# Forming C times the S5 coefficients in the GLA layer, and one memory tile of the S5 layer at the GLA layer's end

## The chip, the cores and the metric

The kernel runs on one core of a Trainium2 chip. The metric is the device time of one execution in microseconds (us); lower is better. The core has five engines with queues of their own: TensorE (PE, with its weight loads shown as PEld), VectorE (DVE), ScalarE (ACT), GpSimd (POOL) and SyncE (SP), which issues most DMAs. PE writes to PSUM (8 banks of 512 f32 columns on 128 partitions), the others work between PSUM and SBUF. They wait for each other through semaphores that are written out by hand in the kernel.

## What is computed

A batch of 256 tokens of width 1024 goes through a first block (attention, mLSTM, a mixture of 32 experts) and then through a second block of two layers, GLA (gated linear attention) and S5 (a diagonal state-space model), each with attention over 256 memory tokens beside it. The change touches the second block. Its reference, cut:

```python
mem_n = rms_norm_2(mem, mem_norm_w)
for i in range(2):                                   # 0: GLA, 1: S5
    h = rms_norm_2(x, norm_w[i])
    seq_out, z, xq = gla_branch(h, ...) if i == 0 else s5_branch(h, ...)
    xa = memory_attention(xq, mem_n, xa_w_kv[i])     # k, v = split(mem_n @ w_kv)
    y = concatenate([seq_out, xa], axis=-1) * silu(z)
    x = x + y @ w_out[i]
...
# s5_branch: u, z, xq = split(h @ w_in)
dt = exp(log_step); mag = exp(lam_re * dt)
ab = mag * (cos(lam_im * dt), sin(lam_im * dt))      # 128 groups x 64 states
coef = (ab - 1) / lam                                # complex
bb = coef * B                                        # B: 64 x 16 per group
x_t = ab * x_{t-1} + bb * u_t
y_t = Re(C x_t) + d * u_t                            # C: 16 x 64 per group
y = gelu(y); y = y * sigmoid(y @ w_glu + b_glu)
```

## The kernel before

The weights of the dense products come in tiles of 2 MB ([128, 4096] f32), numbered in order of use and streamed by SP through a ring of three slots (`RING`); tile n may be loaded once `tile_done` says that tile n - 3 has been used. The ranges of the numbers are `T_GLA` (14 tiles), `T_GLA_OUT` (6), `T_S5` (16), `T_GLU` (8), `T_S5_OUT` (6). Each stage is a `Block` with one hand-written program for each engine; at its end all engines meet at a barrier.

**GLA layer (`stage_gla_layer`).** Most of its input projection and all of the output projections are made as Strassen products: a tile is 7 products of 4 matmuls, and an engine forms sums of quarters of the weight tile first (`sum_weights`, four 128x1024 operations; POOL does so for the input tiles, DVE for the output tiles) and sums of the rows (`dve_rows`, four 128x512 operations). A matmul instruction of the program shows as two in the profile. Behind the input tiles come halves of tiles by plain products (`half`, lines L1846), each 16 matmul instructions into one PSUM bank (6 or 7), taken out by ACT. DVE normalises and gates the attention output (`normalise`, L2126; the gating, L2143), PE turns it (L188), DVE copies it out (L2149). Then the memory attention: scores (L1949), maxima and exponentials, scaling of p by DVE (L2162), turning of p (L1957), its product with `vm` (L1964), multiplication into `zT` (L2169). Between these PE runs the six tiles of the output projection (`out.pe_tile`, L1686). Tiles 2 and 3 need the row sums of the third k block, which DVE can form only after the memory attention. DVE forms the weight sums of tiles 2 to 5 in this stretch, and between those of tiles 3 and 4 it computes the S5 coefficients (`a["decay"]`, `a["turns"]`, `a["coef"]`, lines L2175 to L2215, 64 columns each) with Exp and Sin from ACT (L2033 to L2037). PE turns `ab` behind tile 4 (L1974), ACT stores it to DRAM (`s5_ab_rows`), and the stage ends with the norm for the next layer: squares on ACT (`act_squares`, L1724), roots on POOL (`pool_rstd`), scaling on DVE (L2222), 16 transposes on PE (L1980), and DVE's multiplication into `hT` (L2227).

**S5 scan (`stage_s5_scan`).** 16 steps q; each handles 8 groups of 16 channels, two time steps folded into one. Beside them PE makes the layer's input projection: 32 halves (16 tiles, of which 4 are keys and values of the memory), two a step, one in steps 14 and 15 (`halves_of`). On PE a step is: `half`, `bu(q + 1)` (input times B, L2354), `skip_product(q)` (L2364), second `half`, `y(q)` (states times C, L2373 and L2377). `y(q)` waits for DVE's rotation (`rotated`) and its masked skip matrix (`skip_ready`, L2501). DVE: rotation of bu by the tables (L2474 to L2477), the next step's `step_in` (L2452 to L2455) and `fraction` (L2442), 8 scans (L2487, L2488), `take_y(q - 1)` (L2461), rotation back (L2492 to L2499), skip mask. ACT makes the tables of sine and cosine and takes out the halves. POOL forms `cb`, C times the coefficients, from raw C: four 128x256 operations and one of 128x512 (L2315 to L2320), double buffered, so that group q waits for `y(q - 2)`. SP loads B (with the broadcast `s5_ab_rows`), C (128 KB) and B by state two steps ahead, in that order, and then the ring's next tile.

## Time and profile before

| | us |
|---|---|
| median of 3 runs | 1561.13 (1558.21 to 1562.0) |
| the profiled execution | 1563.43, span 1561.7 |
| mean granted TensorE clock | 0.991 |
| GLA layer | 760 to 1080 |
| S5 scan | 1080.58 to 1363.20 |
| S5 output stage | 1363.20 to the end |

Busy shares of the span: PE 97%, PEld 63%, DVE 44%, ACT 19%, POOL 11%. The first block takes the first 760 us. Read a row of the timeline as: start from the span's start, length of the merged group, engine, line, operation, output and inputs, shapes, count, and in brackets the engine's idle time ahead of it with what ended it. Ends of matmuls are modelled, so a start is surer than an end. PE's granted clock is 1.00 (2.4 GHz) nearly everywhere; 0.50 is 1.2 GHz.

### The profile page before, as it was taken

To read this page: it belongs to the slowest core of one execution; us is meant where nothing else is said; L and a number is where in the kernel's file an instruction comes from. 1 tells how busy PE (TensorE), PEld (TensorE's weight loads), DVE (VectorE), ACT (ScalarE), POOL (GpSimd) and SP (SyncE) were. 2 spreads that over 40 slices of the span, in tenths; PEclk is the share of its full clock that TensorE was granted. 3 is DMA by queue.
4 is the path that set the end of the run, shared out by engine and by line. 5 is a ranking of instruction groups with operands and counts; after the bars stand their busy time and mean duration, and the time that the engine had idled before them with its cause. 6 is when DMAs were issued, how large, how long until landed. Compare 5 with 4: busy or idle time off the path is not lost. (4 is left out here: it accounts for less than half of the span.)

```text
span 1561.7 us, 22744 instructions
## 1 busy us (share of the span) xinstructions
PE 1508.0 (97%) x9125; PEld 989.6 (63%) x9125; DVE 692.0 (44%) x1313; ACT 289.7 (19%) x556; POOL 169.3 (11%) x161
## 2 busy tenths in 40 slices
PE   6999999999999999999999999998999999899998
PEld 2475655344444434433478688887888887488887
DVE  2544324111111111111633333473788888895663
ACT  2222202111111211111120030101223232230000
POOL 0000000000000000000636420002121122000000
PEclk9999999999999999999999999999999999999999
DMA  9544639899999999999333244244454344233441
GB/s 399 213 162 162 254 126 418 337 421 422 422 422 422 422 422 422 422 422 423 118 126 144 108 162 161 109 149 151 142 185 148 136 173 162 111 123 134 164 167 48
DMA packets 53890, 376.05 MB, mean 241 GB/s; under 512 B 7216, under 2 KB 18224, under 8 KB 19264
## 3 DMA queue, kind: packets, MB, share of 16 engines
q1 hardware_dynamic: 53536, 374.02, 60.3%
q8 instruction: 46, 0.75, 0.2%
q10 hardware_dynamic: 288, 1.11, 0.2%
q14 instruction: 20, 0.16, 0.0%
HBM read 373.99 MB, written 1.11 MB: 240 GB/s over the span
## 5 line engine op out<-in xcount | busy, mean ns | idle before, releaser
L1246 PE MATMUL ps<-ring,x_gathered 128*64 128x512 f32 x1024 | 227.9, 597 | 1.0 <-DVE x_gathered L1311 0.9
L1320 DVE TENSOR_TENSOR act_slots<-gate,ps 64x512 f32<-64x512 f32 x32 | 22.1, 690 | 381.3 <-ACT gate L1284 381.3
L2340 PE MATMUL ps<-hT,ring 128*128 128x256 f32 x768 | 172.4, 383 | 2.4 <-PEq L115 2.4
L1246 PEld LDWEIGHTS ps<-ring,x_gathered 128*64 128x64 f32 x1024 | 73.9, 138 | 148.9 <-issue 147.1
L2340 PEld LDWEIGHTS ps<-hT,ring 128*128 128x128 f32 x768 | 145.3, 192 | 23.8 <-issue 4.6
L1269 PE MATMUL ps<-ring,act_turned 128*64 128x512 f32 x512 | 116.9, 598 | 0.0
L1269 PEld LDWEIGHTS ps<-ring,act_turned 128*64 128x64 f32 x512 | 33.9, 136 | 79.1 <-issue 54.8
L1224 PE MATMUL ps<-y,selT 64*128 64x512 f32 x264 | 75.0, 634 | 0.7 <-ACT y L1290 0.7
L261 PE MATMUL ps<-ring,hT 128*128 128x512 f32 x160 | 69.8, 593 | 0.0
L1686 PE MATMUL ps<-ring,zT 128*128 128x256 f32 x288 | 67.4, 380 | 1.9 <-DVE glu_by_token L1548 1.3
L1213 PEld LDWEIGHTS ps<-sel,h 128*128 128x128 bf16 x1584 | 48.4, 98 | 29.1 <-issue 26.0
L1686 PEld LDWEIGHTS ps<-ring,zT 128*128 128x128 f32 x288 | 54.2, 190 | 10.3 <-DVE glu_by_token L1548 1.7
L1379 POOL TENSOR_SCALAR end_stat<-end_ss 128x1 f32<-128x1 f32 x2 | 0.9, 469 | 516.8 <-ACT ring L1369 516.8
L1846 PE MATMUL ps<-hT,ring 128*128 128x256 f32 x256 | 55.7, 379 | 0.0
L1213 PE MATMUL ps<-sel,h 128*128 128x64 bf16 x1584 | 52.3, 194 | 2.4 <-DVE sel_weighted L1301 2.4
L1284 ACT ACTIVATE gate<-ps 64x512 f32<-64x512 f32 x32 | 18.9, 591 | 187.6 <-PE ps L1246 187.6
L2442 DVE SCALAR_TENSOR_TENSOR s_sin<-const,s_turns,s_sin 128x128 f32<-128x128 f32 x64 | 42.8, 727 | 23.1 <-ACT s_sin L2405 23.1
L261 PEld LDWEIGHTS ps<-ring,hT 128*128 128x128 f32 x160 | 29.9, 190 | 35.8 <-issue 35.8
L1846 PEld LDWEIGHTS ps<-hT,ring 128*128 128x128 f32 x256 | 48.5, 190 | 6.5
L1290 ACT COPY y<-ps 128x512 f32<-128x512 f32 x32 | 18.7, 586 | 132.4 <-PE ps L1269 132.4
L280 PE MATMUL ps<-ring,crep 128*32 128x512 f32 x192 | 26.5, 675 | 11.4 <-DMA ring<-in_weights 11.4
L1591 PE MATMUL ps<-ring,hT 128*128 128x256 f32 x144 | 34.6, 383 | 1.4 <-DVE o_sq L1622 1.4
(637 smaller groups left out, 2383.8 us busy)
## 6 DMA issues: line engine op xcount, KB each, us to landing
ring<-in_experts SPq DMA_DIRECT2D x192, 1024.0 KB, 17.1
ring<-in_weights SPq DMA_DIRECT2D x75, 2048.0 KB, 7.7
b_raw<-in_s_b SPq DMA_DIRECT2D x16, 128.0 KB, 7.2
s_a_rows<-s_ab_rows SPq DMA_DIRECT2D x64, 32.0 KB, 6.6
c_raw<-in_s_c SPq DMA_DIRECT2D x16, 128.0 KB, 6.2
b_by_state<-in_s_b_by_state SPq DMA_DIRECT2D x16, 128.0 KB, 2.0
x<-in_x ACTq DMA_DIRECT2D x1, 1024.0 KB, 5.0
mix_room<-in_mem SPq DMA_DIRECT2D x1, 1024.0 KB, 13.9
```

Source lines behind the costliest of these rows:

```text
L261: last = pe.matmul(bank, src[:, kk, h * P:(h + 1) * P], w[:, kk, :], start=(kk == 0), stop=(kk == KD - 1))
L280: last = pe.matmul(bank[32 * j:32 * j + 32, :], crep[:, 2 * j + i, :], w[:, 2 * j + i, :], start=(i == 0), stop=(i == 1), skip_group_check ...
L1213: last = pe.matmul(xg_ps[:, f, :], a["h2"][:, t, part, f * P:(f + 1) * P], sel[:, t, :], start=(t == 0 and part == 0), stop=(t == TT - 1 a ...
L1224: last = pe.matmul(acc[:, t, n, :], selT[rows, b, t * P:(t + 1) * P], y[rows, :], start=False, stop=stop, skip_group_check=True)
L1246: last = pe.matmul(h_ps[rows, :], xg[:, f, :], w[:, kk, m, :], start=(f == 0), stop=(f == KD - 1))
L1269: last = pe.matmul(y_ps[rows, :], act_t[:, f, :], w[:, kk, n * 512:(n + 1) * 512], start=(f == 0), stop=(f == 3))
L1320: dve.tensor_tensor(act_s[:], gate[:], h_ps[upper, :], ALU.mult).then_inc(act_ready, 1)
L1591: last = pe.matmul(self.ps(bank, h), rows[:, kk, :], w[:, kk, :], start=(start and h == 0 and kk == 0), stop=(kk == 3), skip_group_check=True)
L1686: last = pe.matmul(self.sum_of(n, p), rows[:, kk, :], w[:, kk, :], start=(first and kk == 0 and self.PLACE[p][1] == 0), stop=(self.ends(i) ...
L1846: last = pe.matmul(bank[:, f, :], w[:, kk, (2 * h + f) * P:(2 * h + f + 1) * P], k.hT[:, kk, :], start=(kk == 0), stop=(kk == KD - 1))
L2340: last = pe.matmul(out[:, f, :], w[:, kk, (2 * h + f) * P:(2 * h + f + 1) * P], rhs[:, kk, :], start=(kk == 0), stop=(kk == KD - 1))
L2442: last = dve.scalar_tensor_tensor(out=sin[b][:, j, :], in0=even, scalar=a["turns"][:, 4 * q + j:4 * q + j + 1], in1=sin[b][:, j, :], op0=A ...
```

## The change

1. The S5 coefficients are computed earlier in the GLA layer: ACT's part before it takes out the plain halves, DVE's around the gating.
2. POOL's work on C moves from the scan into the GLA layer, behind its weight sums. Raw C is loaded in three DMAs: 1 MB into `hT` when the last input tile is done, and two of 512 KB into parts of `gla_v` after the memory attention. POOL writes to four buffers, and ACT stores each group (256 KB) to DRAM (`s5_c_bar`). In the scan SP loads the finished groups into three buffers.
3. The tile order changes: the first key tile of the S5 layer becomes tile `T_S5`, and its two halves run at the GLA layer's end (`keys_half`), one ahead of the transposes, one behind. ACT takes them out.
4. The scan has 30 halves: two a step, one in steps 3, 7, 11 and 15. `y(q - 1)` stands behind the first half of step q; the rotated states are double buffered, and DVE's `take_y` stands behind the wait for the skip product.

```diff
-T_GLU = T_S5 + 16
+T_S5_SCAN = T_S5 + 1
+T_GLU = T_S5_SCAN + 15
...
             def _(sp):
-                stream(k, sp, T_END_FIRST, T_S5)
+                stream(k, sp, T_END_FIRST, T_GLA_OUT)
+                for h, q in ((0, 0), (1, 8), (2, 12)):
+                    n = 8 if h == 0 else 4
+                    if h == 1:
+                        load(T_GLA_OUT + RING)
+                        sp.wait_ge(xa_out, 1)
+                    sp.dma_start(c_raw[h], k.dram["s5_c"][q:q + n].rearrange("q p j c g -> p q j c g")).then_inc(c_in[h], 16)
+                for n in range(T_GLA_OUT + RING + 1, T_S5_SCAN + RING):
+                    load(n)
                 sp.wait_ge(ab_out, 16)
+                for b in range(4):
+                    sp.wait_ge(c_out[b], 16 * 4)
...
             def _(pe):
+                def keys_half(i, bank):
+                    out, w = k.ps[:, bank, :].rearrange("p (f t) -> p f t", f=2), k.slot(T_S5)
+                    for f in range(2):
+                        for kk in range(KD):
+                            last = pe.matmul(out[:, f, :], w[:, kk, (2 * i + f) * P:(2 * i + f + 1) * P], k.memT[:, kk, :],
+                                             start=(kk == 0), stop=(kk == KD - 1))
+                    return last
...
                 out.pe_tile(pe, 5)
+                k.wait_tile(pe, T_S5)
+                keys_half(0, 1).then_inc(keys_done, 1)
                 pe.wait_ge(ab_copied, 1)
                 for j, t in enumerate((1, 0)):
                     pe.wait_ge(s5_scaled, j + 1)
+                    if t == 0:
+                        pe.wait_ge(keys_out, 1)
...
+                pe.wait_ge(out.added, 4)
+                keys_half(1, 4).then_inc(k.tile_done, 1)
...
             def _(act):
-                out.act_squares(act, 0)
+                for q in range(16):
+                    if q == 10:
+                        out.act_squares(act, 0)
+                    act.wait_ge(c_ready, q + 1)
+                    act.dma_start(k.dram["s5_c_bar"][q], c_bar[:, q % 4].rearrange("p c e j g -> p (c e j g)")).then_inc(c_out[q % 4], 16)
                 act.wait_ge(ab_turned, 1)
...
                 out.act_squares(act, 1)
+                for i, (bank, sem, value) in enumerate(((1, keys_done, 1), (4, k.tile_done, T_S5 + 1))):
+                    act.wait_ge(sem, value)
+                    act.activation(kmT[:, 2 * i:2 * i + 2, :], k.ps[:, bank, :].rearrange("p (f t) -> p f t", f=2),
+                                   ACT.Copy).then_inc(keys_out, 1)
...
             def _(pool):
+                pool.wait_ge(coef_ready, 1)
+                for q in range(16):
+                    pool.wait_ge(c_in[0 if q < 8 else q // 4 - 1], 16)
+                    b = q % 4
+                    if q >= 4:
+                        pool.wait_ge(c_out[b], 16 * (q // 4))
...
+                    pool.tensor_tensor(c_bar[:, b, 0], c_re, cr, ALU.mult)
+                    pool.tensor_tensor(c_bar[:, b, 1], c_re, neg_ci, ALU.mult)
+                    pool.tensor_tensor(c_tmp[:, 0], c_im, neg_ci, ALU.mult)
+                    pool.tensor_tensor(c_tmp[:, 1], c_im, neg_cr, ALU.mult)
+                    pool.drain()
+                    pool.tensor_tensor(c_bar[:, b], c_bar[:, b], c_tmp[:], ALU.add).then_inc(c_ready, 1)
+                    pool.drain()
                 out.pool_rstd(pool)
...
 def stage_s5_scan(k, a):
-        halves_of = [[2 * q + 2, 2 * q + 3] for q in range(14)] + [[30], [31]]
+        starts = [2 + 7 * (q // 4) + 2 * (q % 4) for q in range(17)]
+        halves_of = [list(range(starts[q], starts[q + 1])) for q in range(16)]
...
-                        sp.wait_ge(cb_ready, q + 1)
+                        if q:
+                            sp.wait_ge(y_done, q)
                         load_c(q + 2)
...
                     half(now[0])
+                    if q:
+                        y(q - 1)
                     if q < N - 1:
                         bu(q + 1)
                     skip_product(q)
                     for i in now[1:]:
                         half(i)
-                    y(q)
+                y(N - 1)
...
                     dve.drain()
-                    if q:
-                        take_y(q - 1)
                     dve.tensor_tensor(e_re, z_re[:], cos[b][:], ALU.mult)
...
                     dve.wait_ge(skip_done, q + 1)
+                    if q:
+                        take_y(q - 1)
                     dve.tensor_tensor(skip[:], k.ps[:, 4 + b, 2 * S:3 * S], own[:], ALU.mult).then_inc(skip_ready, 1)
```

The instructions as they stand in a row on the engines, at three places. PE at the GLA layer's end, before: the last products, the 16 transposes of the normalised rows (`gla_v`), and the scan's first two halves.

```order
L1686 MATMUL ps<-exp_k,zT 128x256 x4
L1686 MATMUL ps<-ring,rows_gla_bias 128x256 x4
L1686 MATMUL ps<-ring,zT 128x256 x4
L1980 MATMUL ps<-const,gla_v 128x128 x16
L1817 UNCONDITIONAL_BRANCH
L2323 UNCONDITIONAL_BRANCH
L2340 MATMUL ps<-hT,ring 128x256 x32
```

And with the change (`memT` are the memory tokens):

```order
L1687 MATMUL ps<-exp_k,zT 128x256 x4
L1687 MATMUL ps<-ring,rows_gla_bias 128x256 x4
L1687 MATMUL ps<-ring,zT 128x256 x4
L1898 MATMUL ps<-memT,ring 128x256 x16
L2015 MATMUL ps<-const,gla_v 128x128 x16
L1898 MATMUL ps<-memT,ring 128x256 x16
L1825 UNCONDITIONAL_BRANCH
```

A half of the key tile stands on each side of the transposes. PE in the scan's last two steps, before: half 30, bu(15), skip(14), y(14), half 31, skip(15), y(15).

```order
L2334 MATMUL ps<-ring,memT 128x512 x8
L2354 MATMUL ps<-uT,ab_bar 128x128 x4
L2354 MATMUL ps<-uT,b_raw 128x128 x4
...
L2364 MATMUL ps<-c_bar,b_by_state 128x128 x2
L2373 MATMUL ps<-uT,skip 128x128
L2377 MATMUL ps<-s_x_re,c_bar 32x128 x8
L2377 MATMUL ps<-s_x_im,c_bar 32x128 x8
L2334 MATMUL ps<-ring,memT 128x512 x8
L2364 MATMUL ps<-c_bar,b_by_state 128x128 x2
```

With the change, from y(13) on:

```order
L2419 MATMUL ps<-uT,skip 128x128
L2423 MATMUL ps<-s_x_re,c_bar 32x128 x8
L2423 MATMUL ps<-s_x_im,c_bar 32x128 x8
L2400 MATMUL ps<-uT,ab_bar 128x128 x4
L2400 MATMUL ps<-uT,b_raw 128x128 x4
...
L2410 MATMUL ps<-c_bar,b_by_state 128x128 x2
L2380 MATMUL ps<-ring,memT 128x512 x16
L2419 MATMUL ps<-uT,skip 128x128
```

Two halves now stand between bu(15) and y(14). POOL in the GLA layer, with the change: the last weight sums, the roots, and the first of 16 groups; before, the roots of the next norm (`pool_rstd`) followed at once.

```order
L1468 TENSOR_TENSOR ring<-ring 128x4x256
L1470 TENSOR_TENSOR zT<-ring,zT 128x1024
L179 TENSOR_SCALAR o_rstd<-o_ss 128x8
L182 TENSOR_TENSOR o_rstd<-o_rstd,const 128x8
L2104 TENSOR_TENSOR c_bar_out<-hT,s_coef 128x256
L2105 TENSOR_TENSOR c_bar_out<-hT,s_coef 128x256
L2106 TENSOR_TENSOR c_tmp<-hT,s_coef 128x256
L2107 TENSOR_TENSOR c_tmp<-hT,s_coef 128x256
L2109 TENSOR_TENSOR c_bar_out<-c_bar_out,c_tmp 128x512
```

The 80 operations stand between the attention's roots and the roots of `pool_rstd`, on which the transposes wait.

## Rows read from the trace of the kernel before

**Rows 1.** PE timeline, GLA end: start, us, engine, line, operation, [idle before <-releaser].

```profile
1075.01 1.07 PE L1980 MATMUL ps<-const,gla_v 128*128 128x128 f32 x8 [1.60 <-DVE gla_v L2222]
...
1080.58 0.67 PE L2340 MATMUL ps<-hT,ring 128*128 128x256 f32 x2 [2.37 <-PEq L115]
```

**Rows 2.** PE timeline in one scan step: y, half tile, next half tile.

```profile
1113.05 0.39 PE L2373 MATMUL ps<-uT,skip 128*128 128x128 f32 x2
...
1114.38 7.17 PE L2340 MATMUL ps<-hT,ring 128*128 128x256 f32 x32
...
1123.16 7.07 PE L2340 MATMUL ps<-hT,ring 128*128 128x256 f32 x32
```

**Rows 3.** PE timeline at the scan's end and the next stage's start.

```profile
1348.51 0.79 PE L2373 MATMUL ps<-uT,skip 128*128 128x128 f32 x2 [4.14 <-DVE skip L2501]
...
1351.10 8.90 PE L2334 MATMUL ps<-ring,memT 128*128 128x512 f32 x16
...
1360.83 0.49 PE L2373 MATMUL ps<-uT,skip 128*128 128x128 f32 x2 [0.39 <-DVE skip L2501]
...
1363.20 7.14 PE L2548 MATMUL ps<-kmT,s_xqT 128*128 128x256 f32 x32 [0.87 <-PEq L2266]
```

**Rows 4.** DVE timeline: starts of steps 0 and 1, last rotation of step 15.

```profile
1097.61 0.69 DVE L2474 TENSOR_TENSOR s_z_re<-ps,s_cos 128x512 f32<-128x512 f32 x1 [10.18 <-PE ps L2354]
...
1110.83 0.69 DVE L2474 TENSOR_TENSOR s_z_re<-ps,s_cos 128x512 f32<-128x512 f32 x1 [0.17 <-issue]
...
1358.88 0.68 DVE L2499 TENSOR_TENSOR s_x_im<-s_x_im,s_t_im 128x512 f32<-128x512 f32 x1
```

**Rows 5.** Windows view, scan start: busy us by engine, PEclk, DMA share, GB/s.

```profile
1082.00:1084.00 2.00, 2.00 (x7) 1.55 (x6) 1.14 (x4) 0.79 (x2) 0.00 (x0) 0.50 0.30 70
```

**Rows 6.** PE timeline: three idle times and the matmuls behind them.

```profile
225.61 1.75 PE L990 MATMUL ps<-memT,ring 128*128 128x256 f32 x7 [1.80 <-PEq L366]
...
760.83 8.77 PE L1841 MATMUL ps<-ring,hT 128*128 128x512 f32 x16 [2.12 <-PEq L115]
...
793.88 2.83 PE L1591 MATMUL ps<-zT,hT 128*128 128x256 f32 x8 [2.92 <-DVE gla_qk L1629]
```

**Rows 7.** Timeline: DVE and POOL operations that overlap, GLA layer and scan.

```profile
769.20 2.83 DVE L1488 TENSOR_TENSOR gla_xqT<-hT 128x512 f32<-128x512 f32 x1
...
816.74 2.35 POOL L1464 TENSOR_TENSOR zT<-ring 128x1024 f32<-128x1024 f32 x1 [7.66 <-PE ps L1591]
...
819.23 3.15 POOL L1466 TENSOR_TENSOR zT<-ring,zT 128x1024 f32<-128x1024 f32 x1
...
820.24 3.22 DVE L2084 TENSOR_TENSOR gla_qk<-gla_qk,gate_state 128x1024 f32<-128x1024 f32 x1
...
1336.89 2.90 DVE L2442 SCALAR_TENSOR_TENSOR s_sin<-const,s_turns,s_sin 128x128 f32<-128x128 f32 x4 [1.49 <-ACT s_sin L2405]
```

**Rows 8.** POOL timeline: first and last operation of one group of c_bar.

```profile
1090.05 0.61 POOL L2315 TENSOR_TENSOR c_bar<-c_raw,s_coef 128x256 f32<-128x256 f32 x1 [0.16 <-issue]
...
1092.53 1.26 POOL L2320 TENSOR_TENSOR c_bar<-c_bar,c_tmp 128x512 f32<-128x512 f32 x1
```

**Rows 9.** Timeline at the GLA output projection, ACT, DVE and PE.

```profile
983.26 0.60 ACT L1988 ACTIVATE gla_xqT<-ps 128x512 f32<-128x512 f32 x1 [6.31 <-PE ps L1846]
...
997.76 2.19 DVE L2162 TENSOR_SCALAR gla_v<-gla_v,xa_rs 128x256 f32<-128x256 f32 x8
...
1003.01 1.91 PE L1957 MATMUL ps<-const,gla_v 128*128 128x128 f32 x16
...
1023.29 0.68 DVE L1488 TENSOR_TENSOR zT<-zT 128x512 f32<-128x512 f32 x1
...
1024.05 1.59 PEld L1686 LDWEIGHTS ps<-ring,zT 128*128 128x128 f32 x8 [0.54 <-issue]
...
1048.89 1.97 PE L1686 MATMUL ps<-ring,zT 128*128 128x256 f32 x8 [0.40 <-DVE exp_q L1469]
```

**Rows 10.** The page's DMA issues: KB each, median us to landing.

```profile
ring<-in_weights SPq DMA_DIRECT2D x75, 2048.0 KB, 7.7
```

## What the change should do to the time

> **What bounds the kernel now.** Read first which engine never rests: in the table of the profile it is TensorE (PE), busy 97% of the span, and what it waits for is what can be won. So the second view is PE's idle time in the GLA layer's end and the S5 scan, the two places that the diff touches. There are two large holes. The first lies between the GLA layer's last product and the scan's first matmul: PE stops at 1073.4 (1075.01 less its 1.60 of idle), turns the normalised rows in two short bursts, and starts the scan at 1080.58 [rows 1]: 7.2 us with little work in them. The second is at the scan's end, where y(14) waits 4.14 us for DVE's `skip` [rows 3]. Inside the scan PE does not wait: y takes 1.33 us (1113.05 to 1114.38), and the half tile behind it, with bu and the skip product, 8.78 (to 1123.16) [rows 2]; half a tile is 6.9 to 7.1 us, so bu and the skip product are 1.7. A step with two halves is then some 17.0 us.
>
> The third view is the granted clock. After the first hole it reads 0.50, the 1.2 GHz level, at 1082 to 1084 [rows 5]. After the second, half(31) takes 8.90 us [rows 3] against 7.07 [rows 2], and y(14) takes 2.59 (1348.51 to 1351.10) against 1.33.
>
> **The GLA layer's front (coefficients moved up).** DVE's block of 64-column operations and ACT's Exp and Sin move from the output projection to the gating. PE there runs half tiles of 6.9 us each and asks for the gated rows later than DVE gives them, so I cost the move at nothing; if that cover failed it would cost at most the 4 us of DVE work put ahead of the gating. ACT's takes of the halves come 2 us late at worst, under the same half tiles.
>
> **One tile leaves the scan.** Two halves, 2 x 6.9 = 13.8 us, go. The sum over the scan stage has one more part, the tail. Before, it lost 4.1 (idle) + 1.3 (y at half clock) + 1.8 (half(31), 8.90 less 7.07) + 0.4 (1360.83) = 7.6 us [rows 3]. After, two halves and y(14) stand between bu(15) and y(15): 0.5 + 2 x 6.9 + 1.3 + 0.5 = 16.1 us, while DVE's last step takes 11.1 (from 1348.5, when it had released PE, to 1359.56) [rows 3, 4]. So DVE's rotation is in time, and only take_y(14) and the skip product's mask, which now stand behind the skip product, are waited for: some 0.9 us, an estimate. Gain of the tail 6.7. Scan stage: 13.8 + 6.7 = **20.5 us less**.
>
> The short steps (3, 7, 11) take PE 17.0 - 6.9 = 10.1 us while a DVE step takes 13.2 (1097.61 to 1110.83) [rows 4]. I still cost them at nothing: y is now behind the next step's first half, so DVE has a full step and a half (25 us after bu) and two steps, one long and one short, give 27 us for 26.4 of DVE. SP's loads: b is issued at the end of a step and used 12 us later, C (now 256 KB) a step and a half ahead.
>
> **The tile's two halves in the GLA layer's end.** From the last product to the scan's first matmul there will be 2 x 6.9 for the halves, 2 x 0.9 for the turns, and then the stage boundary behind a PE and ACT finish, which at the layer's start shows 2.12 us of idle [rows 6], with 0.2 for hand-overs: 17.9 against 7.2, so **10.7 us more**. The clock fall at the scan's start stays: after the 2.12 us at 760.83 the 16 matmuls took 8.77 us, where such a half takes 7.1.
>
> **C times the coefficients on POOL.** One group took 1090.05 to 1093.79, with the drain 3.9 us [rows 8]; 16 groups are 62 us. They can't begin before the raw C has landed in `hT`, which is free at 983.3 (the last take) [rows 9]; a 2 MB tile is ahead of it, at 7.7 us [rows 10], and 1 MB more lets me set 994 (bounds 991 and 1002). So POOL works from 994 into the 1070s, beside DVE's weight and row sums.
>
> That isn't free. DVE's operation on two SBUF tensors at 769.20 took 2.83 us [rows 7], the same 512 columns 0.68 at 1023.29 [rows 9]; at 820.24 one of 1024 columns took 3.22, while POOL's at 819.23 was stretched from the 2.35 of the one at 816.74 to 3.15 [rows 7]. Start and end times show turns: DVE waits until POOL's operation has ended, then POOL waits for DVE. Against short c_bar operations four small DVE operations took 2.90 us, 0.73 each [rows 7]. The Trainium skill (SBUF — State Buffer, Who interferes with whom) has the rule behind it: the port pair of VectorE and GpSimd is an exclusive lock, held for the whole instruction, when the DVE operation has two SBUF inputs or runs in a 2-port mode. By its "whole instruction" POOL would lose every such DVE operation in full; the row at 819.23 shows 0.8 us lost for one of 1.2. By the rule the sixteen weight-sum operations would move POOL's end, below, from 1074 to about 1079, still inside its cover; the sum goes by the row.
>
> On PE's path this has three prices. (a) The eight scalings of p: 8 x 0.73 = 5.8 from 997.76 is 1003.6, PE wants them at 1003.01 [rows 9]: **0.6** (bounds 0 and 2.5). (b) The four row sums before tile 2: PE already waits for their end (1023.29 + 0.68, PE at 1024.05 with 0.54 of idle) [rows 9], so all of it lands. Each waits for one POOL operation, a fifth of 3.75 us, less what overlaps: 4 x 0.6 = **2.4** (bounds 0, and 4 x 2.15 = 8.6 by the row at 769.20; POOL's operations are a quarter as long here, so I stay near the low end). (c) PE is then idle 2.9 us. Idle of 1.80 us left the clock alone, 2.12 and 2.92 were followed by a fall [rows 6], and a fall cost 1.7 to 1.8: **1.8** (bounds 0 and 3.1, the two losses behind the second hole). The weight sums: 4 x (1.1 + 0.75) = 7.4 us against 4.9; DVE no longer does the 10 us of coefficients between them, PE's tiles are 12 us apart, and even 9 us would hide. The 0.4 us that tile 4 waited for DVE [rows 9] goes. Together 0.6 + 2.4 + 1.8 - 0.4 = **4.4 us more**.
>
> POOL's end: 994 + 62 + 16 weight-sum operations x 0.8 to 1.0 + some 3 for the rest, about 1074. ACT's queue holds the copy of `ab` and the last squares behind the sixteenth store, and POOL's own roots come behind its last group; PE needs these at about 1085 (1073.4 + 4.4 + 6.9), and they take some 4 us, an estimate. So the last group may end at 1081: 7 us of cover.
>
> **Sum.** -20.5 + 10.7 + 4.4 = -5.4 us. The profiled execution took 1563.43 us for a span of 1561.7, 2.3 above the median of 1561.13; the change should take it to 1558.0 and the median to **1555.7 us**.
>
> **Rivals.**
> *The port costs PE nothing* (C lands late, or the turns fall well): the 2.4, 0.6 and 1.8 are gone, 10.2 less in all: 1550.9. Against it: the row sums have no cover at all. A half-way case, the port without the clock fall, is 1553.9.
> *POOL is late, slower than before.* If the last group ends after 1081, each us delays ACT's copy, the squares and the roots, and with them the turns and the scan. It decides from 1081 and eats the whole gain at 1086 to 1087, that is at 5.8 us a group from 994, where I expect 5.0; at 1092 the kernel takes 1566.7. For it: 3.9 us is the time with DVE quiet, and each store must have left before a buffer is used again. Against it: 7 us of cover.
> *Short steps wait for DVE.* If ACT's tables (which wait for PE's half) hold DVE up in the short steps, PE stands still 2 to 4 us at up to four places: the tail's gain of 6.7 is given back and 2 more: 1564.
> *The change doesn't do what it says*: PE's hole is filled, but the scan isn't shorter, since DVE bounds it. Against it: a DVE step of 13.2 us stands against a mean of 15.3 for PE (three long steps, one short). It is counted in the case before.
>
> **Chances.** Forecast with its half-way case 0.60; port free 0.17; POOL late 0.13; short steps 0.10. A measurement tells about 0.3% (4.7 us) from no change. The forecast lies just beyond that: of its 0.60 some 0.38 is faster by more, 0.22 within. With the port-free case faster is 0.55. Of the two slow cases, 0.23, a mild half (0.11) stays within; so same 0.33, slower 0.12. The range takes in the port-free case with 1.4 us beyond it and the milder part of the slow ones: 1549.5 to 1561.5.
>
> **What would show it.** Tile 2 of the output projection starts some 3 us later, with 2.5 to 3.5 us of PE idle before it and a clock of 0.50 behind. DVE's 128x512 row sums there take 1.2 to 1.4 us each, its 1024-column sums 1.8. POOL's last group ends between 1070 and 1080. From the last product to the scan's first matmul 18 us; the scan stage 262 us instead of 282.6 (1080.58 to 1363.20 [rows 1, 3]), with no PE wait but 1 us before y(15). I am wrong if PE waits for `ab_copied` or the scaled rows by several us, if PE waits in steps 3 to 12, or if DVE's row sums keep their 0.68 us.

## The result and the profile after

The changed kernel takes 1546.12 us (median of 4 runs, 1544.83 to 1548.01), beside 1559.67 for the kernel before in the same comparison: a ratio of 0.9907, 95% interval 0.9894 to 0.9919, so 14.5 us faster by the ratio. A second measurement of the same pair (after_again, below) gave 0.9899, 0.9882 to 0.9916. The forecast was 5.4 us, and 1555.7 us with a range from 1549.5: the sign was right, the size was not.

The two profiled executions differ by more than the medians, by 18.0 us of span (1561.7 and 1543.7). So the first step is to cut the span where both kernels do the same. Three points serve: the first matmul of the GLA layer's memory scores, the scan's first matmul, the first matmul of the S5 output stage.

| us | before | after | difference | forecast |
|---|---|---|---|---|
| start to the scores | 983.91 | 980.41 | -3.50 | 0 |
| scores to the scan's first matmul | 96.67 | 107.33 | +10.66 | +15.1 |
| scan | 282.62 | 257.48 | -25.14 | -20.5 |
| output stage to the end | 198.50 | 198.48 | -0.02 | 0 |

The first line is not the change's. 3.3 us of it are there at the first large product, 36 us into the program, where no line differs. PE timeline of the first 40 us, before:

```profile
33.84 5.23 PE L411 MATMUL ps<-hT,w_gate 128*4 128x256 f32 x32 [1.60 <-DVE hT L699]
39.00 20.87 PE L261 MATMUL ps<-ring,hT 128*128 128x512 f32 x48
```

and after:

```profile
32.13 3.62 PE L412 MATMUL ps<-hT,w_gate 128*4 128x256 f32 x32 [1.60 <-DVE hT L700]
35.69 20.87 PE L262 MATMUL ps<-ring,hT 128*128 128x512 f32 x48
```

The same 32 matmuls took 5.23 and 3.62 us: in one execution the clock was still at its lower level. The 980 us ahead of the scores varied by 8.7 us in the twelve executions below (975.21 to 983.91). The S5 coefficients, moved up in the GLA layer, cost PE nothing, as forecast: from the layer's first product to the scores it is 223.08 us before (760.83 to 983.91) and 223.11 after (757.30 to 980.41). The change's own share of the profiled pair is 10.66 - 25.14 - 0.02 = -14.5 us, and this is what the rest explains. Lines of the changed kernel are numbered 1 to 48 higher.

**The GLA layer's end** (PE timeline), against [rows 1]: the key tile's halves stand on both sides of the transposes.

```profile
1070.04 7.07 PE L1898 MATMUL ps<-memT,ring 128*128 128x256 f32 x32
1076.95 2.01 PE L2015 MATMUL ps<-const,gla_v 128*128 128x128 f32 x16
1078.79 7.07 PE L1898 MATMUL ps<-memT,ring 128*128 128x256 f32 x32
1087.74 14.05 PE L2386 MATMUL ps<-hT,ring 128*128 128x256 f32 x64 [1.88 <-PEq L116]
```

From the end of the last product to the scan's first matmul it is 1087.74 - 1070.2 = 17.5 us. Behind the 1.88 us of idle the clock did not fall: 64 matmuls took 14.05 us. The windows view (length, busy us and count by engine, PEclk, DMA share, GB/s) of the stretch that answers to [rows 5] reads 1.00:

```profile
1088.00:1090.00 2.00, 2.00 (x11) 1.74 (x11) 0.23 (x1) 1.66 (x5) 0.00 (x0) 1.00 0.89 369
```

**The port**, against [rows 9]. DVE timeline: scalings of p, then the four row sums before tile 2.

```profile
994.26 5.07 DVE L2264 TENSOR_SCALAR gla_v<-gla_v,xa_rs 128x256 f32<-128x256 f32 x8
...
1017.65 0.69 DVE L1484 TENSOR_TENSOR gla_xqT<-zT 128x512 f32<-128x512 f32 x1
1018.41 0.95 DVE L1486 TENSOR_TENSOR gla_xqT<-gla_xqT,zT 128x512 f32<-128x512 f32 x1
1019.44 0.95 DVE L1488 TENSOR_TENSOR gla_xqT<-zT,gla_xqT 128x512 f32<-128x512 f32 x1
1020.31 1.10 DVE L1489 TENSOR_TENSOR zT<-zT 128x512 f32<-128x512 f32 x1
```

PE's turning of p began at 999.50, right behind its matmuls. What is left of the port on PE's path is one wait, ahead of tile 2 (PE timeline, before):

```profile
1024.08 1.97 PE L1686 MATMUL ps<-ring,zT 128*128 128x256 f32 x8 [0.16 <-issue]
```

and after:

```profile
1021.51 1.97 PE L1687 MATMUL ps<-ring,zT 128*128 128x256 f32 x8 [1.10 <-issue]
```

**POOL's end** (POOL timeline: last operation of the last group, last root):

```profile
1069.62 1.27 POOL L2109 TENSOR_TENSOR c_bar_out<-c_bar_out,c_tmp 128x512 f32<-128x512 f32 x1
...
1075.00 0.55 POOL L182 TENSOR_TENSOR gla_out_rstd<-gla_out_rstd,const 128x1 f32<-128x1 f32 x1
```

The second half of the rows was scaled at 1076.33 (DVE, 1075.58 and 0.75 us); PE wanted it at 1077.9, in the middle of the transposes.

**The scan.** PE timeline of one long step, against [rows 2]:

```profile
1111.62 13.98 PE L2386 MATMUL ps<-hT,ring 128*128 128x256 f32 x64
1125.43 0.39 PE L2419 MATMUL ps<-uT,skip 128*128 128x128 f32 x2
...
1126.77 0.51 PE L2400 MATMUL ps<-uT,ab_bar 32*128 32x128 f32 x8
...
1128.44 13.98 PE L2386 MATMUL ps<-hT,ring 128*128 128x256 f32 x64
```

The step is 1128.44 - 1111.62 = 16.82 us, where it was 1131.40 - 1114.38 = 17.02. A short step is 9.9 us. PE does not wait in any of them; it waits once, before y(15), where [rows 3] had 4.14 us before y(14):

```profile
1342.85 0.49 PE L2419 MATMUL ps<-uT,skip 128*128 128x128 f32 x2 [0.77 <-DVE skip L2549]
```

### The profile page after: what moved, and what is told of

Its sections match the earlier page's. It is cut to its first block and busy times, and to the rows that moved or that the text cites. A ratio compares the mean times of both kernels' runs of the same rounds, so it can differ in the third digit from the quotient of the medians.

```text
span 1543.7 us, 22762 instructions
## 1 busy us (share of the span) xinstructions
PE 1496.5 (97%) x9125; PEld 987.0 (64%) x9125; DVE 680.3 (44%) x1313; ACT 293.9 (19%) x559; POOL 184.2 (12%) x161
## 3 DMA queue, kind: packets, MB, share of 16 engines
q10 hardware_dynamic: 2592, 5.31, 0.9%
HBM read 378.19 MB, written 5.31 MB: 248 GB/s over the span
## 5 line engine op out<-in xcount | busy, mean ns | idle before, releaser
L2386 PE MATMUL ps<-hT,ring 128*128 128x256 f32 x768 | 168.3, 379 | 1.9 <-PEq L116 1.9
L1868 PE MATMUL ps<-hT,ring 128*128 128x256 f32 x256 | 55.7, 379 | 0.0
```

What stands on the lines that cost most here:

```text
L1868: last = pe.matmul(bank[:, f, :], w[:, kk, (2 * h + f) * P:(2 * h + f + 1) * P], k.hT[:, kk, :], start=(kk == 0), stop=(kk == KD - 1))
L2386: last = pe.matmul(out[:, f, :], w[:, kk, (2 * h + f) * P:(2 * h + f + 1) * P], rhs[:, kk, :], start=(kk == 0), stop=(kk == KD - 1))
```

## Experiments

First theory, from these rows: 14.5 = 5.4 forecast + 9.1, and the 9.1 are 4.1 of the port's price that PE never paid, 1.7 of a clock fall at the scan's start that did not come, 2.9 in the scan, where 14 steps of before lost 0.2 us each, and 0.3 at the GLA end. The rival for each: that the term was small by luck of one execution, or that something else gave the time.

Whole times are too coarse for this: the part before the scores varies. So each experiment is judged by its stages in the trace. They repeat well, as the two executions of the changed kernel show (after_again is the same kernel once more). Each is a difference of three start times of PE's timeline and the span, in us. The last two columns are of whole executions; before was measured anew beside each group of kernels.

| kernel | scores at | scores to scan | scan | output stage | median | ratio to before, interval |
|---|---|---|---|---|---|---|
| before | 983.91 | 96.67 | 282.62 | 198.50 | 1559.67 to 1561.93 | 1 |
| after | 980.41 | 107.33 | 257.48 | 198.48 | 1546.12 | 0.9907 (0.9894 to 0.9919) |
| after_again | 978.30 | 107.34 | 257.48 | 198.48 | 1543.81 | 0.9899 (0.9882 to 0.9916) |
| bu_first | 983.07 | 107.37 | 260.10 | 199.16 | 1551.72 | 0.9936 (0.9919 to 0.9952) |
| both_ahead | 982.20 | 107.78 | 259.18 | 198.44 | 1549.31 | 0.9914 (0.9898 to 0.9931) |
| no_c | 982.92 | 106.39 | 257.49 | 199.60 | 1547.52 | 0.9903 (0.9886 to 0.992) |
| late4 | 982.18 | 112.96 | 257.49 | 198.47 | 1552.38 | 0.9939 (0.9922 to 0.9956) |
| order_only | 975.21 | 96.70 | 278.49 | 200.30 | 1557.73 | 0.9981 (0.997 to 0.9992) |
| keys_back | 981.19 | 100.13 | 278.48 | 200.60 | 1562.76 | 1.0005 (0.9995 to 1.0014) |
| c_in_scan | 982.92 | 106.35 | 266.58 | 199.95 | 1553.82 | 0.9947 (0.993 to 0.9963) |
| combo | 980.16 | 106.43 | 258.78 | 198.83 | 1544.72 | 0.989 (0.9874 to 0.9907) |
| combo2 | 978.95 | 105.75 | 257.10 | 198.80 | 1544.12 | 0.9892 (0.9876 to 0.9909) |

Where the output stage took over 199 us, its first product took 8.8 to 10.2 us instead of 7.14 (1363.20 in [rows 3]), a clock at the lower level behind 0.86 us of idle; that part is in none of the kernels' edits.

### bu_first: a half tile followed by bu again

```diff
                     half(now[0])
-                    if q:
-                        y(q - 1)
                     if q < N - 1:
                         bu(q + 1)
                     skip_product(q)
+                    if q:
+                        y(q - 1)
```

> The changed kernel, with y(q-1) moved behind bu(q+1) and the skip product, so that each scan step again goes from a half tile straight to bu. Theory (a half tile followed by bu takes 7.11 us, followed by y 6.91, so the new order saved 14 x 0.2 us that the forecast missed): the scan stage grows by 2.8 us, and the wait before y(15) from 0.8 to 1.3 us, since the skip product no longer covers it: 3.3 us slower than the changed kernel, some 1549.4 us. Rival (what counts is how often PE changes between half tiles and short products, which is the same in both): only the 0.5 us of the wait, 1546.6 us.

The scan took 260.10 us, 2.6 more than with the change. PE timeline of a long step:

```profile
1131.24 14.08 PE L2386 MATMUL ps<-hT,ring 128*128 128x256 f32 x64
1145.25 0.51 PE L2400 MATMUL ps<-uT,ab_bar 32*128 32x128 f32 x8
...
1146.92 0.39 PE L2419 MATMUL ps<-uT,skip 128*128 128x128 f32 x2
```

Two halves from 1131.24 to 1145.25 are 14.01 us, where the changed kernel's took 13.81 (1111.62 to 1125.43), and the step is 17.01 us (to 1148.25) again. The number of changes between half tiles and short products is the same in both kernels, so the rival falls: it is the neighbours that matter. The last two halves of this kernel tell the two neighbours apart, since they stand behind y(13) and ahead of the skip product:

```profile
1331.61 14.00 PE L2380 MATMUL ps<-ring,memT 128*128 128x512 f32 x32
1345.45 0.61 PE L2410 MATMUL ps<-c_bar,b_by_state 128*128 128x128 f32 x4
```

They take 13.84 us from start to start; the two of this shape between y and bu take 13.93 (1314.68 to 1328.61), and those between the skip product and y in the changed kernel 13.73 (1326.30 to 1340.03). So y ahead costs 0.1 us and bu behind another 0.1. The expectation's "followed by bu" is half of it. This order has 13 places with both, not the 14 of the expectation: 13 x 0.2 = 2.6. The expected 0.5 us more before y(15) did not come (0.87 us of idle against 0.77).

### both_ahead: the last idle time a half us longer

```diff
                 keys_half(0, 1).then_inc(keys_done, 1)
+                pe.wait_ge(out.added, 4)
+                keys_half(1, 4).then_inc(k.tile_done, 1)
                 pe.wait_ge(ab_copied, 1)
...
-                pe.wait_ge(out.added, 4)
-                keys_half(1, 4).then_inc(k.tile_done, 1)
```

> The changed kernel, with both halves of the key tile ahead of the 16 transposes. PE works without a break until the transposes end, then waits for DVE's multiplication into hT and the stage boundary, as before the change: about 2.4 us of idle instead of 1.88. Theory (the length of the last idle time decides whether the granted clock falls; it did after 2.12 us and more, not after 1.88): the clock reads 0.50 behind it, the stretch from the scan's first matmul to bu(0) takes 15.7 us instead of 13.98, together 2.2 us slower than the changed kernel, some 1548.3 us. Rival (before the change the clock fell because PE had worked only 2 of the 7 us ahead): no fall, 0.5 us slower, 1546.6 us.

PE timeline, GLA end:

```profile
1085.68 1.91 PE L2017 MATMUL ps<-const,gla_v 128*128 128x128 f32 x16
1089.98 15.74 PE L2386 MATMUL ps<-hT,ring 128*128 128x256 f32 x64 [2.39 <-PEq L116]
```

PE had worked without a break, and with 2.39 us of idle the clock fell: 15.74 us against 14.05, and the stages grew by 0.45 and 1.70 us. So sparse work ahead, as before the change, is not needed for a fall. That the length of the idle time decides is not isolated by this: here the transposes stand right ahead of it, in the changed kernel a half tile. The half tile behind the transposes saves 2.2 us beyond filling the hole, 1.7 of them the clock.

### no_c: what POOL's work cost the others

```diff
-                    pool.tensor_tensor(c_bar[:, b, 0], c_re, cr, ALU.mult)
...
-                    pool.tensor_tensor(c_bar[:, b], c_bar[:, b], c_tmp[:], ALU.add).then_inc(c_ready, 1)
+                    if q < 4:
+                        pool.memset(c_bar[:, b], 0.0).then_inc(c_ready, 1)
+                    else:
+                        pool.sem_inc(c_ready, 1)
```

> The changed kernel without POOL's 80 operations on C in the GLA layer (C times the coefficients is left out; four buffers are set to zero and stored in its place), so it prices what they cost the others. Theory (the port costs PE only the 0.9 us before tile 2 of the output projection): DVE's four row sums take 0.69 us each, PE's idle before tile 2 is back at 0.2 us, everything else stays: 0.8 to 1.0 us faster than the changed kernel, about 1545.2 us. By the forecast's price of 4.4 us it would be 1541.7 us.

PE timeline at tile 2:

```profile
1023.09 1.97 PE L1687 MATMUL ps<-ring,zT 128*128 128x256 f32 x8 [0.16 <-issue]
```

DVE timeline, the third row sum:

```profile
1021.70 0.69 DVE L1488 TENSOR_TENSOR gla_xqT<-zT,gla_xqT 128x512 f32<-128x512 f32 x1
```

The stretch from scores to scan is 0.94 us shorter, the scan is the same to 0.01 us. The whole price of 62 us of POOL work beside DVE was 0.9 us on PE's path. The median (1547.52, where about 1545.2 was expected) doesn't show it: a difference of 0.9 us is inside the spread of the part before the scores.

### late4: how much cover POOL's end has

```diff
-                    pool.tensor_tensor(c_tmp[:, 0], c_im, neg_ci, ALU.mult)
-                    pool.tensor_tensor(c_tmp[:, 1], c_im, neg_cr, ALU.mult)
+                    for again in range(2 if q >= 12 else 1):
+                        if again:
+                            pool.drain()
+                        pool.tensor_tensor(c_tmp[:, 0], c_im, neg_ci, ALU.mult)
+                        pool.tensor_tensor(c_tmp[:, 1], c_im, neg_cr, ALU.mult)
```

> The changed kernel, with two more POOL operations of 128x256 in each of the groups 12 to 15 (c_tmp is computed twice, same values), so that the last group ends some 5 us later, at about 1076 us. By the forecast's step on POOL's end (cover to 1081, which is 1077.5 in the changed kernel's own times) nothing happens: 1546.1 us. By the changed kernel's trace the cover is 1.6 to 2.1 us only (second rows scaled at 1076.33, needed at 1077.9): PE waits some 3 us before the transposes, 3.3 us slower; if the clock falls behind that wait, 1.7 more: 1549.4 to 1551.1 us.

PE timeline, GLA end:

```profile
1082.23 1.06 PE L2015 MATMUL ps<-const,gla_v 128*128 128x128 f32 x8 [3.32 <-DVE gla_v L2285]
1083.67 1.97 PE L2015 MATMUL ps<-const,gla_v 128*128 128x128 f32 x8 [0.38 <-DVE gla_v L2285]
1085.43 7.83 PE L1898 MATMUL ps<-memT,ring 128*128 128x256 f32 x32
```

The last group ended at 1077.9, 5.2 us later once the 1.8 us are taken off by which the scores were later in this execution. Less the 1.6 us of cover that the changed kernel's rows show, that is 3.6 us. PE waited 3.3 + 0.4 us before and between the transposes, and behind that the second eight transposes took 1.97 us instead of 1.06 and the half tile 7.83 instead of 7.07: 5.6 us in all, a little over the expectation's 3.3 to 5.0. The forecast's 7 us of cover were not there. POOL's C work is within 2 us of being the bound.

### order_only, keys_back, c_in_scan: the parts one at a time

order_only is the kernel before with the scan's new order and nothing else:

```diff
-        x_re, x_im = (sb(f"s5_{x}", [P, 4, S + 1]) for x in ("x_re", "x_im"))
+        x_re, x_im = (sb(f"s5_{x}", [P, 2, 4, S + 1]) for x in ("x_re", "x_im"))
...
                     half(now[0])
+                    if q:
+                        y(q - 1)
...
-                    y(q)
+                y(N - 1)
```

> The kernel before with one part of the change alone: the scan's order (y(q-1) behind the first half of step q, rotated states double buffered, take_y behind the skip product, a third buffer for C). 32 halves, C on POOL in the scan, nothing moved in the GLA layer. Theory: 14 changes from a half tile straight to bu go, 14 x 0.2 = 2.8 us; at the end one half instead of none stands between bu(15) and y(15)'s wait, which I expect at 2.5 us of idle with a clock fall behind, in place of the 7.6 us lost before: 3.8 us won there, less 1.7 if the fall reaches the output stage. The scan stage 6.6 us shorter (276.0), the kernel 4.9 to 6.6 us faster than before. By the forecast's terms, without the 2.8, it would be 2.1 to 3.8 us.

The scan took 278.49 us, 4.1 less. The steps are 16.82 us, as with the change, so the 2.8 us are there. At the end the expectation missed: PE waited not 2.5 but 5.12 us (PE timeline, y(15)).

```profile
1346.87 0.80 PE L2373 MATMUL ps<-uT,skip 128*128 128x128 f32 x2 [5.12 <-DVE skip L2503]
```

I had let DVE start its last step with bu(15), at 1331.2. It started at 1335.66, 4.5 us later, when its step before had ended. In that step DVE had waited for a table from ACT (DVE timeline), which ACT makes behind its take-out of a half, at 1323.16:

```profile
1325.69 1.14 DVE L2444 SCALAR_TENSOR_TENSOR s_sin<-const,s_turns,s_sin 128x128 f32<-128x128 f32 x4 [2.00 <-ACT s_sin L2407]
```

A group of POOL's stands beside that step too, but it isn't the cause: in keys_back, below, POOL does nothing in the scan, and DVE starts its last step 4.5 us behind bu(15) all the same (1345.06 and 1340.57), with 3.05 us of waiting for ACT in the step before. In the changed kernel it is 4.5 us as well (1329.12 and 1324.63), and the two half tiles in front of y(15) cover that; one half tile does not.

keys_back is the changed kernel with the key tile in the scan (`T_S5_SCAN = T_S5`, 32 halves, no `keys_half`):

```diff
-T_S5_SCAN = T_S5 + 1
-T_GLU = T_S5_SCAN + 15
+T_S5_SCAN = T_S5
+T_GLU = T_S5_SCAN + 16
...
-        halves_of = [list(range(starts[q], starts[q + 1])) for q in range(16)]
+        halves_of = [[2 * q + 2, 2 * q + 3] for q in range(14)] + [[30], [31]]
...
-                keys_half(0, 1).then_inc(keys_done, 1)
```

> The changed kernel with the key tile back in the scan: 32 halves there (two a step, one in steps 14 and 15), none at the GLA layer's end. Theory: the GLA end is 10.4 us shorter, the scan has 13.8 us more for the halves, 1.7 for the clock fall at its start (idle of some 2.4 us again) and 3.0 to 4.7 at its end (2.5 us of idle before y(15) with a fall behind it, instead of 0.8): 8.1 to 9.8 us slower than the changed kernel, some 1555.5 to 1557.2 us. If the move of the tile paid only by its fill of the hole (13.8 less 10.4 = 3.4): 1550.8 us.

PE timeline, GLA end and scan end:

```profile
1075.80 3.60 PE L2011 MATMUL ps<-const,gla_v 128*128 128x128 f32 x16 [4.76 <-DVE gla_v L2272]
1081.32 15.74 PE L2375 MATMUL ps<-hT,ring 128*128 128x256 f32 x64 [1.91 <-PEq L116]
...
1356.27 0.80 PE L2408 MATMUL ps<-uT,skip 128*128 128x128 f32 x2 [5.12 <-DVE skip L2538]
...
1359.80 10.19 PE L2585 MATMUL ps<-kmT,s_xqT 128*128 128x256 f32 x32 [0.87 <-PEq L2317]
```

It is as slow as the kernel before (1.0005), where the expectation had at most 1557.2 us. Two costs were missing in it. Without the tile the roots behind POOL's last group are waited for, 4.76 us, and the clock falls behind that, so that the GLA end is only 7.2 us shorter. And the scan's end loses, as in order_only, 4.3 us of idle (5.12, where the changed kernel has 0.77) and 1.2 us of y(15) at the lower clock (2.66 us instead of 1.51). With the two halves (13.8) and the fall at the scan's start (1.7) that makes the 21.0 us by which the scan is longer. The clock is still down at the output stage (10.19 us), 2.1 more. So the tile's move is worth 13.8 us in these two stages, where its fill of the hole alone is 3.4: it also covers POOL's late end and DVE's last step.

c_in_scan is the changed kernel with POOL's work on C in the scan:

```diff
-                        if q:
-                            sp.wait_ge(y_done, q)
+                        sp.wait_ge(cb_ready, q + 1)
                         load_c(q + 2)
...
+            @block.gpsimd
+            def _(pool):
+                for q in range(N):
+                    b = q % 2
+                    pool.wait_ge(c_in[b], 16 * (q // 2 + 1))
+                    if q >= 3:
+                        pool.wait_ge(y_done, q - 2)
```

> The changed kernel with POOL's work on C left in the scan, as before the change (three buffers, group q waits for y(q-3)); the key tile at the GLA end and the short steps stay. Theory: a long and a short step together take PE 26.7 us, two DVE steps of 13.2 take 26.4, so PE waits 0 to 2 us in the whole scan; tile 2 of the output projection gets its 0.9 us back: 0.9 faster to 1.1 slower than the changed kernel, 1546.5 to 1548.5 us. Rival (the move of C is what makes the short steps possible, DVE would not keep up): 2 to 3 us of waits in each of steps 4, 8, 12 and more at the end, 8 us slower, 1555.4 us.

The rival was right. DVE timeline in the scan with C there:

```profile
1191.79 0.77 DVE L2525 TENSOR_TENSOR_SCAN s_z_re<-s_decay,s_z_re 128x128 f32<-128x128 f32 x1
1192.48 1.48 DVE L2526 TENSOR_TENSOR_SCAN s_z_im<-s_decay,s_z_im 128x128 f32<-128x128 f32 x1
1193.89 0.39 DVE L2525 TENSOR_TENSOR_SCAN s_z_re<-s_decay,s_z_re 128x128 f32<-128x128 f32 x1
```

and the same operation in the changed kernel:

```profile
1185.97 0.40 DVE L2535 TENSOR_TENSOR_SCAN s_z_re<-s_decay,s_z_re 128x128 f32<-128x128 f32 x1
```

Beside POOL's group (1188.92 to 1193.69) the 128x128 scans take up to 0.77 and 1.48 us instead of 0.40, and the DVE step 16.5 us (1183.85 to 1200.32) instead of the 13.9 of the changed kernel (1178.46 to 1192.40); in neither does DVE wait for another engine. DVE's steps are 15.8 us on average here (fifteen from 1104.62 to 1341.79), where PE's would be 15.1, so DVE bounds the scan, and PE (its timeline) waits in the middle and at the end:

```profile
1232.50 0.49 PE L2409 MATMUL ps<-uT,skip 128*128 128x128 f32 x2 [1.45 <-DVE skip L2539]
...
1237.47 0.81 PE L2390 MATMUL ps<-uT,ab_bar 32*128 32x128 f32 x8 [3.46 <-DVE ab_bar L2493]
...
1353.00 0.49 PE L2409 MATMUL ps<-uT,skip 128*128 128x128 f32 x2 [2.22 <-DVE skip L2539]
```

The scan is 9.1 us longer: 7.1 of waits where the changed kernel has 0.8, and most of the rest is PE at the lower clock behind them (bu's rows of 0.51 us take 0.81 at 1237.47). The GLA part is 1.0 shorter. The 13.2 us of [rows 4], on which my expectation stood, belong to step 0, beside which POOL does nothing.

### combo and combo2: edits that follow from the reading

```diff
+                act.activation(a["vm"][:, 1, 512:1024], k.ps[:, 7, :], ACT.Copy).then_inc(vm_taken, 1)
                 tiles.act_p1(act, 1)
...
+                act.activation(a["kmT"][:, 2:4, :], k.ps[:, 4, :].rearrange("p (f t) -> p f t", f=2),
+                               ACT.Copy).then_inc(keys_taken, 1)
                 numbers(0)
...
+                    if q == 6:
+                        pool.wait_ge(out.rows_ready[2], 1)
...
+                    if q == 15:
+                        out.act_squares(act, 1)
                     act.wait_ge(c_ready, q + 1)
...
-                    if q:
+                    if 0 < q < N - 1:
                         take_y(q - 1)
```

> The changed kernel with four small edits that follow from the reading. ACT's last take-out in the stages ahead of the GLA layer and ahead of the scan is done at the start of the next stage, so that PE, not ACT, ends the stage: idle at the GLA start from 2.12 to some 1.5 us, and by the theory on the clock no fall behind it (8.8 us for the first half becomes 7.1), 2.3 us; idle at the scan's start from 1.88 to some 1.3, 0.6 us. POOL pauses while DVE forms the row sums before tile 2: 0.9 us; the squares stand ahead of ACT's last store, so that POOL's later end (1072 instead of 1070.9) is not felt. DVE's mask ahead of take_y in the last step: 0.4 us. Together 4.2 us faster than the changed kernel, about 1543.2 us. Rival (the clock falls at the GLA start whatever the last idle time is, or the boundary is as long without ACT's take-out): 1.3 to 1.9 us faster.

combo2 adds one edit:

```diff
-                for n in range(T_GLA_OUT + RING + 1, T_S5_SCAN + RING):
+                for n in range(T_GLA_OUT + RING + 1, T_S5_SCAN + RING - 1):
                     load(n)
...
+                load_tile(RING - 1)
                 load_b(0)
```

> The kernel of four edits, and one more: SP's load of the scan's third ring tile, which SP issues only when PE has ended the GLA stage (0.3 us), is moved to the start of the scan. Theory (that DMA issue, the last work of the stage on any engine, kept the boundary at 1.90 us where the one ahead of the GLA layer, without such a load, shrank to 1.50): idle at the scan's start 1.5 us, and no clock fall behind it: 13.98 instead of 15.67 us to bu(0). 2.1 us faster than the kernel of four edits, about 1542.5 us, 0.9876 of before. Rival (the boundary does not shrink, since it waits for something else): idle 1.9 us, the same time as the kernel of four edits, 0.989.

PE timeline of combo at the scan's start:

```profile
1086.59 15.74 PE L2388 MATMUL ps<-hT,ring 128*128 128x256 f32 x64 [1.90 <-PEq L116]
```

SP's timeline of combo, the last load of the stage, issued when PE had ended:

```profile
1084.71 0.33 SPq L1829 DMA_DIRECT2D ring<-in_weights  x1
```

PE timeline of combo2 at the GLA layer's and the scan's start:

```profile
757.53 7.10 PE L1862 MATMUL ps<-ring,hT 128*128 128x512 f32 x16 [1.50 <-PEq L116]
...
1084.70 14.05 PE L2389 MATMUL ps<-hT,ring 128*128 128x256 f32 x64 [1.23 <-PEq L116]
```

The idle at the GLA start went from 2.12 to 1.50 us and the first half took 7.10 us instead of 8.80. Tile 2 waits 0.17 us, y(15) 0.39 (0.38 in combo). Only the edit at the scan's start failed at first: in combo the idle there stayed at 1.90 us, where 1.3 was expected, and the clock fell behind it; with SP's load moved it is 1.23 and nothing falls. From the boundary ahead of the GLA layer (757.30 less 2.12 in after, 757.53 less 1.50 here) to the output stage combo2 takes 585.8 us, the changed kernel 590.0: 4.3 us less. Yet the medians measured side by side are 1544.12 (combo2) and 1543.81 (after_again), ratios 0.9892 and 0.9899 with intervals that overlap nearly whole. So a gain of combo2 over the change is seen in the stages and not shown in the time.

### after_again: does the clock's hold repeat

> The changed kernel once more, on the chip and beside the runs of the kernel before that the next one shares. The median 13 to 15 us under before, as before. In the trace: idle of 1.88 us at the scan's start. If the clock held there by the length of the idle time, the stretch to bu(0) takes 13.98 us again; if that was luck of one execution, 15.7 us may show now.

PE timeline, the scan's start:

```profile
1085.64 14.05 PE L2386 MATMUL ps<-hT,ring 128*128 128x256 f32 x64 [1.88 <-PEq L116]
```

It repeated, with every stage behind the scores within 0.01 us. The median was 17.3 us below that of before, 15.8 by the ratio, where 13 to 15 were expected. So the hold of the clock was not luck of one execution. But the margin is thin: combo lost the clock at the same place behind 1.90 us.

## Why the prediction was right in sign and wrong in size

The step that failed most is the port's price on PE's path: the forecast had 4.4 us there, the trace has 0.3. Two more terms stood at nothing and were 2.9 us (the half tiles' neighbours in the scan) and 1.7 us (the clock fall that did not come). With 0.3 at the GLA end these are the 9.1 us by which the gain was undersized.

- **The coefficients' move, at nothing: right** (223.08 and 223.11 us from the layer's first product to the scores).
- **GLA end, 10.7 us more: right.** It was 17.5 - 7.2 = 10.4. The boundary's idle was 1.88 us, where I had taken 2.12.
- **Two halves out of the scan, 13.8 us: right**, and the **tail, 6.7: right**, with 0.77 us of idle before y(15) where 0.9 was forecast.
- **The scan's steps: a term was missing, 2.9 us.** The half tile between y and bu takes 7.17 us (7.11 to the next start, 1114.38 to 1121.49), the one between the skip product and y 7.07 (6.91, 1106.14 to 1113.05); [rows 2] holds 7.17 and 7.07. I read "6.9 to 7.1" as a spread and put the difference into "bu and the skip product are 1.7". The new order has no half tile of the first kind in steps 1 to 14. bu_first puts them back and loses 2.6 us.
- **"The clock fall at the scan's start stays": wrong, 1.7 us.** I took it over from the boundary at 760.83. That one has 2.12 us of idle, the new one 1.88, and the forecast itself had the row of 1.80 us without a fall. both_ahead (2.39, fall) and after_again (1.88, none) fit the length as the cause, but combo fell behind 1.90, and 2.12 was not always followed by a fall. So this 1.7 us could not have been read off the rows before, and that it was won is in part luck.
- **The port, 4.4 us: mis-sized; it was 0.3.** (a) The scalings of p took 0.63 us each, near the 0.73 of the step, but they ended 0.2 us before PE wanted them: 0 instead of 0.6. (b) The first row sum kept its 0.69 us, the other three took 0.95 to 1.10, not 1.28: 0.9 instead of 2.4 (no_c). The forecast had turns of whole operations in it; the start times show 1.03 us a turn at most, where a DVE operation (0.69) and a POOL operation (0.61) alone are 1.30. The Trainium skill (SBUF — State Buffer, SBUF: two separate sides) has the pair of ports locked for the whole instruction; here some 0.27 us of each pair of operations overlapped. (c) A fall of the clock behind 2.9 us of idle hung on (b), and on 0.54 us of idle before that were the weight load's in [rows 9], where PE's matmuls had 0.16; the idle was 1.1 us: 0 instead of 1.8. The wait at tile 4 went, as forecast, and was worth 0.6 from start to start, not 0.4. 0.9 - 0.6 = 0.3, 4.1 us less than the sum had.
- **The cover of POOL's end: wrong, without effect on the time.** The last group ended at 1070.9, which is the forecast 1074 less the 3.5 us that this execution was ahead. But the chain behind it (copy of ab, squares, roots, scaling; 1070.89 to 1076.33) took 5.4 us and not 4, and PE came 4.1 us earlier, since the port cost it nothing. The cover was 1.6 us, and late4 ran through it.
- **What the move of C was good for** was not in the forecast at all: it is counted there only as a cost. The rival "short steps wait for DVE" is what would have come without it, and c_in_scan shows it, at 9.1 us in the scan.

The sum again with what was measured: scan -25.1, GLA end +10.4, port +0.3, together -14.4; the profiled pair gave -14.5 in these stages, the two ratios give -14.5 and -15.8. The chances had 0.17 for "the port costs nothing", at 1550.9; even that case lacked the clock and the step, so the range's lower end was too high by 3.4 us. These two small terms made up half of the miss; the step's was readable in rows that were on the table, the clock's was not.

## What to carry to other kernels

Where a trace shows two values for the same instruction, ask which neighbour makes the difference before calling it a spread: times the number of steps, it is a term. Price the contention of two engines by what is waited for at that place, not by the sum of what both lose: 62 us of POOL beside DVE cost 0.9 where DVE had cover, and the same work in the scan, where it had little, 9.1. And when single executions differ, cut the span at points common to both kernels; the same kernel's stages behind the scores repeat to 0.01 us here while the whole varies by 5.

## What the runs showed of the hardware

- **Idle time and the clock.** At the scan's start, in twelve executions: idle of 1.23 us and of 1.82 to 1.88 us (seven executions) left PE's clock at 2.4 GHz, 1.90 (combo) and 2.37 to 2.39 (three) were followed by 1.2 GHz. (In keys_back it was already down.) The 1.80 us of [rows 6] were followed by no fall in any of the twelve. At the GLA start 2.12 us was followed by a fall in eight executions of ten, and by none in both_ahead and order_only; 1.50 us by none in two. So near 2 us the outcome is not the idle time's alone, and what else decides was not found; of 0.87 us ahead of the output stage, with short products around it, a slow first product followed in five of twelve, three of them with a clock fall shortly before. A fall costs 1.7 us where a half tile follows.
- **The first 980 us took 975 to 984 us.** Part of it is the clock: 32 matmuls at 32 us took 3.62 us in one execution and 5.05 to 5.31 in the others, and the first 32 of the experts, behind 0.93 us of idle, 7.09 or up to 9.90 us. That was not followed further.
- **A stage boundary is held by the last engine, issue of a DMA included.** With ACT's last 0.60 us moved behind the boundary, PE's idle there went from 2.12 to 1.50; at the other boundary it did not change until SP's 0.33 us issue moved as well, and then went from 1.90 to 1.23.
- **DVE's scans take turns with POOL too**: 128x128 in 0.68 to 1.48 us instead of 0.40.
- **A half tile's time depends on its neighbours**: y ahead of it and bu behind it cost 0.1 us each (bu_first).
